# Router with low parts and rows' statistics moved between engines, in a Fourier-mixer and mixture-of-experts trunk

## The reference

```python
def fourier_mixer(x, w_in, w_out):
    u = (x @ w_in).reshape(B, S, N_FOURIER_GROUPS, FOURIER_GROUP_DIM)
    f = jnp.fft.fft2(u.astype(jnp.float32), axes=(1, 3), norm='ortho').real
    return f.reshape(B, S, D_MODEL).astype(x.dtype) @ w_out
...
y = fourier_mixer(x, fourier_w_in[j], fourier_w_out[j])
x = layer_norm(DEEPNORM_ALPHA * x + y, ln_g[i, 0], ln_b[i, 0])
y = grouped_moe(x, router_w, router_b, expert_w_gate[i], expert_w_up[i], expert_w_down[i])
x = layer_norm(DEEPNORM_ALPHA * x + y, ln_g[i, 1], ln_b[i, 1])
```

## Time and profile before

| | |
|---|---|
| median of three runs | 2222.4 us (2217.44 to 2226.54) |
| the profiled execution | 2222.27 us |
| its span in the profile | 2220.2 us |
| what lies around the span | 2.1 us |
| TensorE, VectorE, ScalarE, GpSimd busy | 93%, 62%, 43%, 27% of the span |
| mean granted TensorE clock | 0.969 |

### The profile page before, as it was taken

The page is one execution under the profiler, slowest core; times in us unless marked ns, Lnnn a source line. Parts: engine busy times, 40 slices in busy tenths (PEclk is TensorE's granted clock), DMA queues, the critical chain, the costliest instruction groups (busy, mean ns, idle before and its releaser), DMA issues.

```text
span 2220.2 us, 38717 instructions
## 1 busy us (share of the span) xinstructions
PE 2070.8 (93%) x12300; PEld 1795.2 (81%) x12301; DVE 1382.7 (62%) x2341; ACT 954.4 (43%) x1446; POOL 601.1 (27%) x600
## 2 busy tenths in 40 slices
PE   8989999999999649999999999999999999999990
PEld 4656778788878539899899999998998999989980
DVE  4342266776687757665666666676666666666644
ACT  3231022122122225554555555555555555555534
POOL 3000012443443521321232232323222322223214
PEclk9999999999999869999999999999999999999995
DMA  7795233434342357867787787888777878878826
GB/s 277 258 270 172 84 119 135 138 118 150 122 142 91 134 168 249 253 204 231 211 258 232 223 245 243 232 261 249 234 239 210 256 228 244 263 226 246 241 69 208
DMA packets 149488, 451.38 MB, mean 203 GB/s; under 512 B 43488, under 2 KB 45536, under 8 KB 145248
## 3 DMA queue, kind: packets, MB, share of 16 engines
q1 hardware_dynamic: 98592, 277.59, 39.2%
q0 software_dynamic: 50848, 173.14, 26.9%
HBM read 337.50 MB, written 117.78 MB: 205 GB/s over the span
## 4 chain that ended last, share of the span: by engine, by line
PE 87%; DVE 4%; issue 3%; DMA 2%; ACT 2%; DVEq 1%; ACTq 0%; POOL 0%; POOLq 0%; SPq 0%
PE ps L980 34%; PE ps L840 16%; PE ps L1008 15%; PE ps L783 4%; PE ps L968 3%; PE ps L825 3%; PE ps L1016 3%; PE ps L881 2%; PE ps L798 2%; PE ps L749 1%; PE ps L868 1%; DMA xch<-x 1%; PE ps L973 1%; ACT L1225 1%; DVE fin_r L1731 1%
## 5 line engine op out<-in xcount | busy, mean ns | idle before, releaser
L1008 PE MATMUL ps<-wd_hi,hidT 128*128 128x512 f32 x1056 | 293.0, 402 | 0.4 <-ACT hidT L1231 0.4
L1513 DVE TENSOR_TENSOR wd_lo<-wraw,wd_hi 128x1024 fp32r<-128x1024 f32 x132 | 161.6, 1225 | 156.7 <-ACT wd_hi L1184 153.0
L1008 PEld LDWEIGHTS ps<-wd_hi,hidT 128*128 128x128 f32 x1056 | 190.0, 188 | 36.3 <-ACT hidT L1231 0.8
L1513 DVE TENSOR_TENSOR wu_lo<-wraw,wu_hi 128x1024 fp32r<-128x1024 f32 x132 | 160.7, 1219 | 52.6 <-ACT wu_hi L1184 48.9
L980 PE MATMUL ps<-mxT_hi,wg_hi 128*128 128x256 f32 (+2 forms) x1056 | 163.5, 298 | 30.2 <-issue 26.9
L980 PEld LDWEIGHTS ps<-mxT_hi,wg_hi 128*128 128x128 f32 x1056 | 145.5, 192 | 43.9 <-issue 31.5
L1134 ACT CAST xt_hi<-ps 128x256 fp32r<-128x256 f32 x128 | 41.4, 375 | 323.1 <-PE ps L825 323.1
L1513 DVE TENSOR_TENSOR wg_lo<-wraw,wg_hi 128x1024 fp32r<-128x1024 f32 x132 | 161.1, 1222 | 29.4 <-ACT wg_hi L1184 29.3
L1872 POOL DMA_INDIRECT sums<-yrow_a,ent_now x33 | 58.3, 1768 | 421.6 <-DVE yrow_a L1589 364.9
L980 PE MATMUL ps<-mxT_lo,wg_hi 128*128 128x256 f32 (+2 forms) x1056 | 158.9, 293 | 0.0
L980 PE MATMUL ps<-mxT_hi,wu_lo 128*128 128x256 f32 (+2 forms) x1056 | 157.2, 291 | 0.0
(11 more groups left out here) (267 smaller groups left out, 4121.3 us busy)
## 6 DMA issues: line engine op xcount, KB each, us to landing
wraw<-expert_w_gate SPq DMA_DIRECT2D x132, 512.0 KB, 5.4
wraw<-expert_w_up SPq DMA_DIRECT2D x132, 512.0 KB, 5.8
wraw<-expert_w_down SPq DMA_DIRECT2D x132, 512.0 KB, 4.3
xch<-x SPq DMA_DIRECT2D x16, 1024.0 KB, 8.8
first_stage<-ych SPq DMA_DIRECT2D x16, 1024.0 KB, 8.9
yt<-first_stage SPq DMA_DIRECT2D x16, 1024.0 KB, 4.9
w_out_s<-fourier_w_out SPq DMA_DIRECT2D x4, 1024.0 KB, 9.2
w_in_s<-fourier_w_in SPq DMA_DIRECT2D x1, 4096.0 KB, 21.7
```

The source lines that it names most:

```text
L1008: mm = nc.tensor.matmul(psY[h], hidT[:, l, c, t * P:(t + 1) * P], wd[r][:, c, cols], start=(i == c == 0), stop=(i == 2 and c == FC - 1))
L1513: nc.vector.tensor_tensor(piece(1, j), wraw[:, j % SLOTS, :], piece(0, j).bitcast(F32), ALU.subtract).then_inc(wlo_ok, 1)
```

## The change

The router is now made with fp32r parts. ScalarE casts the transposed rows (`hT[0]`), VectorE takes their low parts (`turn_lo`, new), and the router matrix is kept as its high and low parts beside each other (`rw2`), so that each of the 8 chunks is two matmuls with 64 stationary columns, one on the high part of the rows and one on the low. The two halves of 32 scores come out on separate partitions and are summed by `turn_scores`, now a product with two identities stacked (`halves`).

The router of g-2 now runs between the two halves of group g's cross product, not at the end of group g-1, and `scores` of g-2 (a copy, the turned scores, and a sigmoid on them) stands at the head of ScalarE's group g. `turn_lo(g-1)` stands on VectorE between `take_ranks` and `rows_cross`. The fourth block of `turn_rows` waits for the first low part, since they share a bank. VectorE's statistics are gone: ScalarE sums each row and the squares (`rows_deviation`), writing the discarded products into `psP`, so that the product waits for `std_ok` where it waited for `p_ev`. `place` runs ahead of `rows_finish`. `yt` and `m2s` have one buffer, and are loaded one second stage later. In the last group, the router and ranks are spread between the passes of the product.

```diff
-        yt_t = at("yt", 144, 4 * D)
+        yt_t = at("yt", 144, 2 * D)
-        hT_t = at("hT", 176, 2 * D)
+        hT_t = [at("hT_hi", 176, 2 * D, F32R), at("hT_lo", 152, 2 * D, F32R)]
...
             def load_group(g, b):
-                sp.wait_ge(xj_ps, s2_base(g - 2) + 4)
+                sp.wait_ge(xj_ps, s2_base(g - 1) + 4)
...
                     if jj < 2 and not is_first(g, 3):
-                        pe.wait_ge(xj_ev, base_j - 1 + jj)
+                        pe.wait_ge(th_lo, 4 * g - 9 + jj)
...
                         if last:
-                            pe.wait_ge(xj_ev, base_j + max(jj - 1, 0))
+                            pe.wait_ge(th_lo, 4 * g + max(jj - 1, 0))
                         elif jj < 3:
                             pe.wait_ge(xj_ev, base_j - 2 + jj)
                             pe.wait_ge(xl_ev, 4 * g + 10 + jj)
                         else:
-                            pe.wait_ge(xj_ev, base_j + 1)
+                            pe.wait_ge(th_lo, 4 * g + 1)
...
+            def router(g, dst=psL):
+
                 for c in range(CH):
                     if c % 4 == 0:
-                        pe.wait_ge(xj_ev, base_j + 2 + c // 2)
-                    mm = nc.tensor.matmul(dst, rwv[:, c, :], hT[:, c, :, :].rearrange("p s n -> p (s n)"),
-                                          start=(c == 0), stop=(c == CH - 1))
+                        pe.wait_ge(th_lo, 4 * g + 2 + c // 2)
+                    for r in range(2):
+                        mm = nc.tensor.matmul(dst, rw2[:, c, :, :].rearrange("p r e -> p (r e)"),
+                                              hT[r][:, c, :, :].rearrange("p s n -> p (s n)"),
+                                              start=(c == r == 0), stop=(r == 1 and c == CH - 1))
                 mm.then_inc(lg_ps, 1)
...
+            def cross_product(g):
+                if not is_first(g):
+                    pe.wait_ge(q_ev, g)
+                product_half(psQ, 1, B, 0, is_first(g))
+                if not is_first(g, 2):
+                    router(g - 2)
+                product_half(psQ, 1, B, 1, is_first(g)).then_inc(q_ps, 1)
...
-                product(g, 1, psQ, B, q_ev, q_ps, edge_row=is_first(g))
+                cross_product(g)
                 if not is_first(g, 2):
                     turn_scores(g - 2)
-                product(g, 0, psP, A, p_ev, p_ps)
+                if not is_first(g):
+                    pe.wait_ge(std_ok, g)
+                product_half(psP, 0, A, 0)
+                product_half(psP, 0, A, 1).then_inc(p_ps, 1)
...
                     turn_rows(g - 1, 1 - b, tr_base(g))
-                    router(g - 1, tr_base(g))
...
+            def scores(g, b):
                 act.wait_ge(lg_ps, g + 1)
-                if not is_first(g):
-                    act.wait_ge(st_ps, g)
-                src = psL2 if isinstance(g, int) and g == GROUPS - 2 else psL
-                nc.scalar.activation(scT, src, ACT.Sigmoid).then_inc(sg_ok, 1)
+                second = isinstance(g, int) and g == GROUPS - 2
+                nc.scalar.copy(scT, psL2 if second else psL).then_inc(sg_ok, 1)
+                act.wait_ge(st_ps, g + 1)
+                nc.scalar.activation(sc2[b].rearrange("p s e -> p (s e)"), psS2 if second else psS, ACT.Sigmoid
+                                     ).then_inc(sc_ok, 1)
+
+            def rows_deviation(g, b):
+
+                act.wait_ge(radd_ok, 2 * g + 2)
+                for s in range(2):
+                    if s:
+                        act.wait_ge(rvar_ok, 2 * g + 1)
+                    nc.scalar.activation(psP[:, :], rows[:, b, s, :], ACT.Identity, scale=-1.0 / D,
+                                         accum_out=rneg[:, s:s + 1]).then_inc(rmean_ok, 1)
+                    act.wait_ge(rmean_ok, 2 * g + s + 1)
+                    nc.scalar.activation(psP[:, :], rows[:, b, s, :], ACT.Square, bias=rneg[:, s:s + 1],
+                                         accum_out=rvar[:, s:s + 1]).then_inc(rvar_ok, 1)
+                act.wait_ge(rvar_ok, 2 * g + 2)
+                nc.scalar.activation(lnstd[:, 0:2], rvar[:, 0:2], ACT.Sqrt, scale=1.0 / D, bias=eps_c
+                                     ).then_inc(std_ok, 1)
...
+            def turn_lo(g, base_j):
+                for jj in range(4):
+                    dve.wait_ge(xj_ev, base_j + jj + 1)
+                    nc.vector.tensor_tensor(hT_dst(1, jj), hT_src(g, jj), hT_dst(0, jj).bitcast(F32), ALU.subtract
+                                            ).then_inc(th_lo, 1)
...
                 if not is_first(g, 2):
                     take_ranks(g - 2)
+                if not is_first(g):
+                    turn_lo(g - 1, tr_base(g))
                 rows_cross(g, b, i)
                 rows_ready(g, b)
-                rows_finish(g, b)
                 if not is_first(g, 2):
                     place(g - 2, b, i - 1)
+                rows_finish(g, b)
...
             rows_cross(g, 1, GROUPS // 2 - 1)
-            choose(g - 2)
+            turn_lo(g - 1, tr_base(g))
+            choose(g - 2, 1)
             take_ranks(g - 2)
             place(g - 2, 1, GROUPS // 2 - 2)
-            choose(g - 1, psS2)
+            choose(g - 1, 0)
             rows_ready(g, 1)
-            rows_finish(g, 1)
             take_ranks(g - 1, psR2)
             place(g - 1, 0, GROUPS // 2 - 1)
+            rows_finish(g, 1)
+            turn_lo(g, tr_base(GROUPS))
```

More of the change, by code:

```diff
@@ L331, in trunk_kernel @@
         payg = [grow.take(f"payg{b}", 12, I32) for b in range(2)]
[L332 to L333 removed]
+        scT = grow.take("scT", 2 * P)[0:2 * E, :]
+        sc2, sel, sel2, eq = [small("sc0", 2, E), small("sc1", 2, E)], *(
+            small(n, 2, E) for n in ("sel", "sel2", "eq"))
         rank, msum = (small(n, 2, LISTS) for n in ("rank", "msum"))
@@ L405, in trunk_kernel @@
         xj_ps, xj_ev = sem("xj_ps"), sem("xj_ev")
-        q_ps, p_ps, q_ev, p_ev = (sem(n) for n in ("q_ps", "p_ps", "q_ev", "p_ev"))
-        var_ok, std_ok, hg_ok, h_ok = (sem(n) for n in ("var_ok", "std_ok", "hg_ok", "h_ok"))
+        q_ps, p_ps, q_ev = (sem(n) for n in ("q_ps", "p_ps", "q_ev"))
+        std_ok, hg_ok, h_ok = (sem(n) for n in ("std_ok", "hg_ok", "h_ok"))
         h_out = [sem("h_out0"), sem("h_out1")]
@@ L506, in last_bank, with hT_src, hT_dst @@
             return psX[1 + jj % 2]
+        def hT_src(g, jj):
+            last = isinstance(g, int) and g >= GROUPS - 2
+            return (last_bank if last else turn_bank)(jj).rearrange("p (c n) -> p c n", c=4)
+        def hT_dst(part, jj):
+            return hT[part][:, 4 * (jj // 2):4 * (jj // 2) + 4, jj % 2, :]
         def s2_src(jj):
@@ L837, in product_half @@
                                              start=(n == 0 and c == 0), stop=False)
-                for n, (l, r) in enumerate(PASSES):
+                for n in passes:
+                    l, r = PASSES[n]
                     for c in range(CH):
@@ L887, in turn_scores @@
                 for s in range(2):
-                    mm = nc.tensor.transpose(dst[:, s * E:(s + 1) * E], scT[:, s * P:(s + 1) * P],
-                                             ident[0:E, 0:E])
+                    mm = nc.tensor.matmul(dst[:, s * E:(s + 1) * E], scT[:, s * P:(s + 1) * P],
+                                          halves[0:2 * E, :], start=True, stop=True)
                 mm.then_inc(st_ps, 1)
@@ L928, in _ @@
             pe.wait_ge(xl_ev, 4 * g + 4)
-            product(g, 1, psQ, B, q_ev, q_ps)
+            cross_product(g)
             turn_scores(g - 2)
             turn_rows(g - 1, 0, tr_base(g))
-            router(g - 1, tr_base(g), psL2)
+            pe.wait_ge(std_ok, g)
+            product_half(psP, 0, A, 0, passes=range(1))
+            router(g - 1, psL2)
+            product_half(psP, 0, A, 0, passes=range(1, 2))
+            turn_scores(g - 1, psS2)
+            product_half(psP, 0, A, 0, passes=range(2, 3))
+            product_half(psP, 0, A, 1, passes=range(1))
             ranks(g - 2)
-            pe.wait_ge(p_ev, g)
-            product_half(psP, 0, A, 0)
-            turn_scores(g - 1, psS2)
-            product_half(psP, 0, A, 1).then_inc(p_ps, 1)
+            product_half(psP, 0, A, 1, passes=range(1, 3)).then_inc(p_ps, 1)
             ranks(g - 1, psR2)
             turn_rows(g, 1, tr_base(GROUPS))
-            router(g, tr_base(GROUPS))
+            router(g)
             turn_scores(g)
@@ L957, in _ @@
             pe.sem_inc(yc_ps, 2)
-            pe.wait_ge(p_ev, GROUPS)
+            pe.wait_ge(std_ok, GROUPS)
             pe.wait_ge(q_ev, GROUPS)
@@ L1159, in group @@
                     empty_turn(tr_base(g), g - 1)
-                    scores(g - 1)
-                act.wait_ge(var_ok, g + 1)
-                nc.scalar.activation(lnstd[:, 0:2], lnmv[:, 0:2, 1], ACT.Sqrt, bias=eps_c).then_inc(std_ok, 1)
+                if last:
+                    scores(g - 1, 1 - b)
+                rows_deviation(g, b)
             empty_s2(0)
```

(4 more changed lines are left out.)

86 lines of the change are left out of this document (38 added, 48 removed).

## The result

The changed kernel takes 2301.75 us (median of 4 runs, 2292.11 to 2308.49), the kernel before 2222.99 beside it (4 runs, 2217.44 to 2226.54). The ratio is 1.0353, with a 95% interval of 1.0310 to 1.0397: slower by 3.5%. The forecast was 2297 us, within 2268 to 2320.

What follows compares the result with a forecast made beforehand. TensorE bounds the 32.47 us round; the change makes its cross product wait for VectorE. First start +1.1, thirteen rounds 68.1 and the end +5.4 give 74.6 us on 2222.27: 2297 us, range 2268 to 2320.

Steps and rivals of the forecast that it cites:

- VectorE's chain takes the router's place as the bound of the seam: Before the cross product: low parts delay `rows_cross`, moving the start from T+10.08 to T+11.2 (T: second stage's start).
- The router: On TensorE: 16 fp32r matmuls at 0.12 us each, 1.92 us in place of 3.57, a gain of 1.65.
- The scores' turn: On TensorE: becomes a float32 product of two matmuls, taken as 0.44 us, bounds 0.24 and twice that.
- A round without the clock: Second-stage round with the cross product starting at T+11.2 and the router still to come: 35.7 us, +3.2.
- The clock: TensorE after some 3.9 us idle: a granted clock of 0.50 in every round, costing 2.0 us, bounds 1.6 to 3.4.
- The rival of a wait without the clock: Low parts and transposes before the cross product's wait might keep TensorE's clock up: 2271 us, chance 0.14.
- Sum of the rounds: Thirteen second-stage rounds at 3.24 us for the wait plus 2.0 for the slow clock: 5.24 each, 68.1 us.
- First round: The first of 14 cross-product starts that wait so, ahead of the thirteen rounds: +1.1 us.
- The end: Last round's new order, from the cross product's start to the first finished row: +5.4 us, bounds +1 and +9.
- ScalarE's statistics at nought: ScalarE's passes done by T+20.1, the product that waits at T+24.4 earliest: cover 4 us, cost nothing.
- The rival on the other side: Cross product starting before T+8.0 makes rounds shorter, by 1.3 us at T+6.7: 2205 us, chance 0.04.
- No change, by cheap low parts: Low parts cost almost nothing on VectorE's chain, cross product at T+8.4, +0.4 a round: 2232 us, chance 0.05.

Runs made afterwards that it cites:

- e4_fill: Changed kernel plus 28 unread 256-column matmuls on TensorE between the transposes and the cross product's wait; 2273.83 us, ratio 1.0217.
- e6_early_ranks: Changed kernel with the ranks of group 13, in the last round, straight behind the turned scores of group 14; 2299.28 us, ratio 1.0330.
- e3_stats_only: Kernel before with only ScalarE's row statistics and `place` ahead of `rows_finish`, router as before; 2225.32 us, ratio 1.0008.
- e7_no_lo: Changed kernel with VectorE's four low-part subtractions left out everywhere, their tile zeroed once; 2237.69 us, ratio 1.0058.
- best1: Changed kernel with `rows_cross` in two separately signalled halves, the first releasing half the cross product, and transposes, low parts, router and last-group ranks moved; 2214.91 us, ratio 0.9954.
- e2_router_seam: Changed kernel with the router of g-1 put back between the transposes and the next cross product; 2248.26 us, ratio 1.0106.
- e1_lo_behind: Changed kernel with the four low parts behind `rows_cross` on VectorE, not ahead of it; 2256.45 us, ratio 1.0129.
- e5_short_lo: Changed kernel with each low part cut to 16 of 512 elements a partition; 2291.26 us, ratio 1.0296.

## Why the prediction was right, step by step

- **VectorE's chain takes the router's place as the bound of the seam.** Right. The cross product starts at T+11.1 (taken: T+11.2); the bounds T+10.9 and T+11.7 hold it. The steps hold one by one: the first low part at T+5.96 (5.95), the fourth at T+8.02 (8.0), the end of `rows_cross` at T+10.96 (11.08).
- **The router.** 16 matmuls from 573.22 to 575.04, 1.82 us (taken 1.92, from a row with 128 stationary columns). 64 stationary columns are no slower: 0.114 each.
- **The scores' turn.** 0.56 us from start to start (580.60 to 581.16), where I took 0.44. This is over my upper bound of twice 0.24. The two transposes before are recorded as two matmuls, 0.12 each; the two float32 products are recorded as four, 0.14 each.
- **A round without the clock.** 35.7 forecast, 35.62 in e4_fill.
- **The clock.** 2.0 forecast in every round; 1.96 on the mean. That it is this near is luck: the 2.0 was picked from rows that spread from 1.6 to 3.4 (the last is 3.3 when the two groups are compared with their times at the full clock). That the clock falls in each round is the part that was forecast, and it is now shown and not only argued: filling the same wait with matmuls gave 28 us back and a granted clock of 1.00 in the rounds. The rival of a wait without the clock (2271) is refuted for the changed kernel, and its time is where e4_fill came out, 2274.
- **Sum of the rounds.** 13 x 5.24 = 68.1 forecast, 66.2 measured. (The forecast's own low bound of -12 adds up to -13; the range does not rest on it.)
- **First round.** +1.1 forecast, +0.5 measured. VectorE has no ranks to take in it, so the cross product at its end starts at T+10.4 and not at T+11.2.
- **The end.** +5.4 forecast, +7.0 measured. The two are not taken to the same mark: the forecast ran to the first finished row, which comes at 51.5 us, +6.3, and 0.7 more follow until the tables' matmul. The mis-sized step is the ranks of group 13: I had them end at 29.7 us, and they end at 31.8 (790.91 to 822.7), since the wait ahead of the last two blocks of transposes (1.47 us) and the slow clock behind it (eight matmuls in 2.74 us) stand ahead of them. e6_early_ranks shows that the ranks carry the end: 3.7 us for this one call's place.
- **ScalarE's statistics at nought.** Right, by e3_stats_only. The passes begin at T+13.5 and the root ends at T+20.0 (567.90 and 574.40, with T at 554.43), as worked out. The cover is 6.8 us and not 4, because the product starts at T+26.7 and not at T+24.4: the slow clock, which I had left out of that sum, delays it.
- **The rival on the other side** (faster, if the cross product may start before T+8.0). The point is borne out from both sides: e7_no_lo at T+8.4 is slower than before, best1 at T+6.5 is faster. For the changed kernel it does not hold, for the reason given: VectorE's order is fixed.
- **No change, by cheap low parts** (T+8.4). Refuted; they cost 2.7 us a round. Cutting their width wins back only 1.0 us of the start, since ScalarE's casts then hold `rows_cross` back.

The loss of 5.11 us a round is thus split by runs: 1.96 the clock (e4_fill), 2.68 the low parts ahead of `rows_cross` (e4_fill against e7_no_lo), 0.47 the rest (e7_no_lo's 32.94 against 32.47), in which the faster router pays back most of the lost cover. The three terms that I summed give 74.6 us and measure 73.7; that they come so near is in part errors of both signs, the rounds 1.9 too high and the end 1.6 too low. The median moved by 78.8; the 5 us between lie outside the rounds and the end, in stretches where profiles of one kernel differ by as much, and I can't assign them.

## What to carry to other kernels

A long operation in front of a wait is also that wait's cover: before it is moved or shortened, see what the other engine's chain to the semaphore takes, and compare the two from the same starting point (here T). An instruction added ahead of the one that signals costs its own time or, where that is longer, the chain that it waits for; making it shorter helps only until that chain takes over. So signal first, or in halves, and do the rest behind. And idle time on TensorE had a second price here, in the clock, which the granted clock of a round shows at once. Cut into pieces it was cheaper: 2.1 us in three pieces (e2_router_seam) lowered the clock in none of 13 rounds, where one wait of 1.8 or 1.9 us in each round (e7_no_lo) did in 3.

## What the runs showed of the hardware that I had not expected

The granted clock is already down while TensorE still stands. In the two us ahead of the changed kernel's last cross product in the loop, TensorE has no matmul, and the mean granted clock is 0.54:

```profile
788.37:790.37 2.00, 0.00 (x0) 0.00 (x0) 2.00 (x3) 0.00 (x0) 1.70 (x2) 0.54 0.10 18
```

The length of one wait did not decide whether the clock fell, within a broad middle: it did behind 3.75 and 3.25 us in each of 13 rounds, behind 2.8 or 2.9 us in 4 of the other 12 rounds of e1_lo_behind and behind the 2.1 of its first, behind 1.9 us in 3 of the rounds of e7_no_lo, each four rounds apart, and behind 1.20 with two shorter pieces before it in none. At the seam that ends e7_no_lo's thirteenth round it fell behind a wait of 1.80 us (0.69 over the four us after it). Rounds of the changed kernel that are alike in every other row differ in how long the lowered clock lasts: the first eight matmuls take 3.75 us in most and 3.07 in every third. In e5_short_lo a shorter wait was followed by a longer stretch of it. The Trainium skill, TensorE: Matmul & The Clock Gate, section "HAM oscillation — how this bites in real kernels", tells of loops that pay the slow clock in each turn; the changed kernel does so in 13 of 13 rounds, e1_lo_behind and e7_no_lo in some only.
